# Waits at eleven phase borders of a three-block kernel follow the data in place of the barrier; first products drawn into the phases before

## The reference, cut to what matters

```python
def first_block(x, mem, ...):
    h = _rms(x, attn_norm_g)
    y_fox, y_lru, y_sb, y_mem = ...            # four mixers of h; y_mem attends to mem
    gates = sigmoid(h @ w_in[:, gates] + b_gate)
    mixed = sum over n of gates[n] * (branch[n] @ w_branch[n])
    x = x + mixed @ w_out
    h2 = _rms(x, ffn_norm_g)
    x = x + (silu(conv(h2 @ w_up_gate)) * (h2 @ w_up_val)) @ w_down

def second_block(x, c, ctx, ...):
    for l in range(2):
        mod = silu(c) @ w_ada[l] + b_ada[l]    # shifts, scales and gates, for x and for ctx
        h = modulate(layernorm(x)), hc = modulate(layernorm(xc))
        f = (g_att * (o_att @ w_att_o) + g_gla * (o_gla @ w_gla_o) + g_conv * (y_conv @ w_conv_o)) @ w_out
        x = layernorm(ALPHA * x + gate * f); the same for a gated feed-forward part
```

## Time and profile before

| | us |
|---|---|
| median of 3 runs | 3212.21 (3208.3 to 3212.28) |
| the profiled execution, its device time | 3214.86 |
| span of its trace | 3213.1 |
| TensorE busy in the span | 3066.1 (95%) |
| VectorE busy | 1624.3 (51%) |
| ScalarE busy | 674.1 (21%) |
| mean granted TensorE clock | 0.984 |

### The profile page before, as it was taken

One profiled execution on the slowest core, in us unless ns is written; L12 is line 12 of the kernel. 1 busy time (PEld: TensorE's weight loads), 2 busy tenths in 40 slices (PEclk: granted clock), 3 DMA queues, 4 the chain that ended last, 5 costly groups with the idle time before them and its releaser, 6 DMA issues. The chain is left out here.

```text
span 3213.1 us, 41219 instructions
## 1 busy us (share of the span) xinstructions
PE 3066.1 (95%) x13794; PEld 2429.4 (76%) x13794; DVE 1624.3 (51%) x3320; ACT 674.1 (21%) x1622; POOL 66.9 (2%) x109
## 2 busy tenths in 40 slices
PE   9999899999998999999999999999989999998998
PEld 8888788878885556667775488888856778887887
DVE  4455226656653357658887244445343565753111
ACT  3334220000003333321112132110043431022001
POOL 0000001100110000000000000000000000000000
PEclk9999899999999999999999999999999999999999
DMA  5243347755761011112221202222211223433443
GB/s 187 93 142 101 125 178 266 265 193 203 255 234 53 2 68 54 61 46 85 85 79 65 90 28 83 89 91 85 85 53 42 69 74 111 150 111 111 150 159 103
DMA packets 104999, 363.21 MB, mean 113 GB/s; under 512 B 11489, under 2 KB 17633, under 8 KB 104801
## 3 DMA queue, kind: packets, MB, share of 16 engines
q1 hardware_dynamic: 90832, 310.92, 28.5%
q0 software_dynamic: 14096, 51.39, 4.5%
HBM read 361.21 MB, written 1.05 MB: 113 GB/s over the span
## 5 line engine op out<-in xcount | busy, mean ns | idle before, releaser
L560 PE MATMUL bank<-H,W 128*128 128x256 f32 (+1 forms) x3616 | 879.8, 401 | 9.2 <-DVEq L305 6.3
L560 PEld LDWEIGHTS bank<-H,W 128*128 128x128 f32 x3616 | 690.8, 192 | 177.9 <-issue 85.9
L560 PE MATMUL bank<-YG,W 128*128 128x256 f32 (+1 forms) x1984 | 525.2, 422 | 7.7 <-ACTq L305 7.5
L560 PEld LDWEIGHTS bank<-YG,W 128*128 128x128 f32 x1984 | 378.0, 191 | 137.6 <-issue 94.4
L1031 PE MATMUL bank<-H,W 128*128 128x512 f32 (+1 forms) x320 | 120.4, 513 | 5.4 <-ACT H L1588 5.4
L1128 PE MATMUL bank<-W,H 128*128 128x256 f32 x512 | 117.1, 379 | 0.0
L1300 ACT ACT_TABLE_LOAD x21 | 26.9, 1283 | 391.3 <-DVEq L305 390.2
L880 PE MATMUL bank<-MX,SQ 128*128 128x256 f32 x480 | 105.2, 379 | 0.0
L1128 PEld LDWEIGHTS bank<-W,H 128*128 128x128 f32 x512 | 94.8, 190 | 13.3 <-issue 1.9
L880 PEld LDWEIGHTS bank<-MX,SQ 128*128 128x128 f32 x480 | 91.2, 190 | 12.4
L1031 PEld LDWEIGHTS bank<-H,W 128*128 128x128 f32 x320 | 60.2, 192 | 49.0 <-issue 43.2
(11 more groups left out here) (425 smaller groups left out, 4316.3 us busy)
## 6 DMA issues: line engine op xcount, KB each, us to landing
W<-stream SPq DMA_DIRECT2D x556, 512.0 KB, 3.3
WORK<-ada POOLq DMA_DIRECT2D x59, 512.0 KB, 4.0
SQ<-ada POOLq DMA_DIRECT2D x28, 512.0 KB, 5.0
W<-stream SPq DMA_DIRECT2D x24, 384.0 KB, 3.2
YG<-ada POOLq DMA_DIRECT2D x9, 512.0 KB, 4.5
W<-stream SPq DMA_DIRECT2D x16, 128.0 KB, 2.4
CN<-consts SPq DMA_DIRECT2D x1, 1984.0 KB, 15.4
X<-x_in SPq DMA_DIRECT2D x2, 512.0 KB, 5.0
```

The source lines that it names most:

```text
L560: m = pe.matmul(out_ap, W[u][:, c, :], src[:, c, cols], start=first and c == 0, stop=last and c == k - 1)
```

## The change

TensorE's list `ahead` gets out1, down1, merge2 0, mix_out, conv_norm 1, merge2 1, out2 and down2 1. In each of these the first tile starts after waits on the data themselves (banks that are free, chunks that are written), and `phase_done` is awaited later in the phase. In up2 of layer 0, already in the list, the wait for the last hidden tiles moves behind the first tile. Two first products move across a border that keeps its barrier: the key tiles of memory_first go into stick_last, ahead of each suffix sum, and merge1's first gate tile goes into memory_last, ahead of the transposition; merge1's turns are rotated to match, with the order of the tiles unchanged. `conv_norm` of layer 1 takes the other layer's body. In memory_first the two small products and the root of the context's layernorm move back; its last step moves to merge1's head. VectorE's ada tiles of down1 all go behind the first output tile of a turn.

```diff
@@ stick, memory
                 for k in range(2):
                     project_pair(s, k)
+                    if not s.projects:
+                        memory_key(Step(tally, plan, s.number + 1, 0), k)
                     if s.attends:
...
+            def memory_key(s, u):
+                if u == 0:
+                    pe.wait_ge(*s.before("k_taken"))
+                project(s, u, bank[0][:, u * S:(u + 1) * S], CTX)
...
-                if s.projects:
-                    pe.wait_ge(*s.before("k_taken"))
+                if not s.projects:
+                    first_gate(Step(tally, plan, s.number + 1, 0, counting=False))
+                if s.projects and s.attends:
                     for u in range(2):
-                        project(s, u, bank[0][:, u * S:(u + 1) * S], CTX)
-                        if u == 0 and not s.attends:
-                            ctx_mean(bank[5], ctx_tmp[0], 3)
+                        memory_key(s, u)
...
                     for u in range(2):
                         project(s, 2 + u, bank[1][:, u * S:(u + 1) * S], XS)
-                    if not s.attends:
-                        ctx_mean(bank[6], ctx_tmp[1], 9)
+                        if u == 0 and not s.attends:
+                            ctx_mean(bank[5], ctx_tmp[0], 3)
...
                         project_tokens(s, 4 + u, ...)
+                    if not s.attends:
+                        ctx_mean(bank[6], ctx_tmp[1], 9)
+
+            def first_gate(s):
+                pe.wait_ge(*s.earlier("k_taken", 0))
+                pe.wait_ge(*s.before("gate0"))
+                project(s, 0, bank[0][:, 0:S], XS)
...
+            def merge1_middle(s, following):
+                merge1_rest(s)
+                first_gate(following)
@@ merge2, out_tiles
-                for j in range(2):
-                    pe.wait_ge(*s.before(f"mixed{j}"))
-                    project(s, j, bank[j][:, 0:T2 - cols.start], cols, src=Y2[2])
+                pe.wait_ge(*s.before("mixed0"))
+                pe.wait_ge(*s.done("loaded0"))
+                for c in range(KC):
+                    pe.wait_ge(*s.earlier("conv_done", KC - 1 - c))
+                    m = pe.matmul(bank[0][:, 0:T2 - cols.start], W[0][:, c, :], Y2[2][:, c, cols],
+                                  start=c == 0, stop=c == KC - 1)
+                m.then_inc(*s.tick("unit"))
+                pe.wait_ge(tally.sem("phase_done"), WORKERS * s.number)
+                pe.wait_ge(*s.before("mixed1"))
+                project(s, 1, bank[1][:, 0:T2 - cols.start], cols, src=Y2[2])
...
+                for name in (("gate0", "mixed0", "gate1", "mixed1") if first else ("mixed0",)):
+                    pe.wait_ge(*s.earlier(name, 0))
+                pe.wait_ge(*s.before("added0"))
+                pe.wait_ge(*s.done("loaded0"))
+                for c in range(KC):
+                    if c == KC - 1:
+                        pe.wait_ge(*s.earlier("mixed3" if first else "mixed1", 0))
+                    m = pe.matmul(bank[0][:, 0:S], W[0][:, c, :], MX[:, c, cols], start=c == 0, stop=c == KC - 1)
+                m.then_inc(*s.tick("unit"))
+                for u in range(1, 4):
+                    if u == 2:
+                        pe.wait_ge(tally.sem("phase_done"), WORKERS * s.number)
@@ mix_out, up2, down
+                        if h + i == 0 and c == KC - 1:
+                            pe.wait_ge(*s.earlier("mixed1", 0))
...
-                for i in range(8):
+                pe.wait_ge(*s.earlier("mixed0", 0))
+                out_tile(0, 0)
+                pe.wait_ge(tally.sem("phase_done"), WORKERS * s.number)
+                for i in range(1, 8):
                     out_tile(0, i)
...
-                for j in range(2):
-                    pe.wait_ge(*s.earlier(f"hidden{j}", 0))
...
                     pe.wait_ge(*s.done(f"loaded{j}"))
+                    if j:
+                        for i in range(2):
+                            pe.wait_ge(*s.earlier(f"hidden{i}", 0))
...
+                    if j:
+                        pe.wait_ge(tally.sem("phase_done"), WORKERS * s.number)
+                    else:
+                        pe.wait_ge(*s.earlier("hidden0", 0))
                     for q in range(3):
                         u = 3 * j + q
+                        if u == 2:
+                            pe.wait_ge(*s.earlier("hidden1", 0))
@@ conv_norm_first
-                for name in ("acc_taken0", "first_taken0", "cross_taken0"):
+                for name in (("gate0", "mixed0", "gate1", "mixed1") if s.layer else ("acc_taken0", "first_taken0", "cross_taken0")):
                     pe.wait_ge(*s.earlier(name, 0))
-                for c in range(3):
+                one, two = (1, 3) if s.layer else (3, 5)
+                for c in range(one):
...
@@ ScalarE: memory, condition; VectorE: condition, down1, layernorm
-                    if not s.attends:
-                        ctx_rstd()
                     rstd_pair(s, (1.0, 256 ** -0.5), "q_taken")
...
+                    if not s.attends:
+                        ctx_rstd()
...
-                act.wait_ge(tally.sem("ctx_norm"), 13)
-                act.activation(H[:, :, CTX], ctx_n, ACT.Copy).then_inc(tally.sem("ctx_norm"), 1)
...
+                dve.wait_ge(tally.sem("ctx_norm"), 12)
+                dve.tensor_tensor(H[:, :, CTX], ctx_n, rows(forget_f[:, :]), ALU.mult).then_inc(tally.sem("ctx_norm"), 1)
...
-                    for k in range(2 * j, 2 * j + 2):
+                    for k in range(4 if j == 0 else 0):
                         ada_tile("down1", s.turn, k)
...
-                        dve.tensor_tensor(cen[:, c, c0:T2], cen[:, c, c0:T2], SQ[:, c, c0:T2], ALU.mult)
+                        dve.tensor_tensor(cen[:, c, c0:T2], cen[:, c, c0:T2], SQ[:, c, c0:T2], ALU.mult)\
+                           .then_inc(*s.tick("conv_done"))
```

More of the change, by code:

```diff
@@ L759, in merge, with merge1_begin, merge1_rest @@
+            def merge1_begin(s):
+                pass
+            def merge1_rest(s):
+                for n in range(4):
+                    if n:
+                        pe.wait_ge(*s.before(f"gate{n}"))
+                        project(s, 2 * n, bank[2 * n][:, 0:S], XS)
                     pe.wait_ge(*s.before(f"mixed{n}"))
-                    project(s, 2 * n + 1, bank[2 * n + 1][:, 0:T2 - cols.start], branches[n][1], src=branches[n][0])
-            def merge1(s):
-                merge(s, [(y, slice(0, S)) for y in Y1], XS, 4)
+                    project(s, 2 * n + 1, bank[2 * n + 1][:, 0:S], CTX, src=Y1[n])
@@ L996, in layernorm @@
                 m.then_inc(*s.tick("mean"))
[L997 to L1003, removed]
-                    mean_square(s, bank[1][:, 0:T2 - c0], slice(c0, T2), "variance")
-                if s.plan[s.number][0] == "conv_norm":
-                    for c in range(first_gates, KC):
-                        if c >= 6:
-                            pe.wait_ge(*s.done("gate_conv", c - 6))
-                        project(s, c, bank[2 + c % 6][:, 0:T2 - c0], slice(c0, T2))
+                mean_square(s, bank[1][:, 0:T2 - c0], slice(c0, T2), "variance")
             def attend(s):
@@ L1281, in conv_norm_first @@
+                for c in range(one, two):
+                    project(s, c, bank[2 + c][:, 0:n], cols)
+                mean_pairs(s, bank[1][:, 0:n], cols)
+                for c in range(two, KC):
                     if c >= 6:
                         pe.wait_ge(*s.done("gate_conv", c - 6))
-                    project(s, c, bank[2 + c % 6][:, :], slice(0, T2))
+                    project(s, c, bank[2 + c % 6][:, 0:n], cols)
             run(pe, {"prepare": prepare, "fox": fox, "lru_in": lru_in,
@@ L1286, in _ @@
                      "stick": stick,
-                     "memory": memory, "merge1": merge1, "out1": out_tiles, "norm_ffn1": norm_ffn1, "up1": up,
-                     "down1": down, "ln_mixer": layernorm, "attend": attend,
-                     "gla": (gla_gates, gla_middle, gla_end), "conv": conv, "conv_norm": layernorm, "merge2": merge2,
+                     "memory": memory, "merge1": (merge1_begin, merge1_middle, merge1_rest), "out1": out_tiles,
+                     "norm_ffn1": norm_ffn1, "up1": up, "down1": down, "ln_mixer": layernorm, "attend": attend,
@@ L1290, in _ @@
+                     "gla": (gla_gates, gla_middle, gla_end), "conv": conv, "merge2": merge2,
                      "out2": out_tiles,
                      "post_mixer": layernorm, "ln_ffn": layernorm, "up2": up2, "down2": down, "post_ffn": layernorm, ("down2", 0): down_strassen,
-                     ("conv", 0): conv_strassen, ("conv_norm", 0): conv_norm_first, "mix_out": mix_out},
-                ahead=[("fox_first", 0), ("conv_norm", 0), ("up1", 0), ("attend_first", 0), ("attend_first", 1), ("up2", 0), ("up2", 1)]
+                     ("conv", 0): conv_strassen, "conv_norm": conv_norm_first, "mix_out": mix_out},
@@ L1294, in _ @@
```

(2 more changed lines are left out.)

30 lines of the change are left out of this document (11 added, 19 removed).

## The result

The changed kernel takes 3176.85 us (median of 4 runs, 3175.86 to 3182.09) against 3211.5 of the kernel before (4 runs): a ratio of 0.9891, 95% interval 0.9879 to 0.9904. The forecast was 3176. Its profiled execution took 3177.3 us with a span of 3175.5. Of the title's eleven borders, nine start on waits for data now; into memory_first and merge1 the barrier stays and a first product has moved ahead of it.

A forecast was written before the change was run, and what follows sets the result against it. TensorE, busy 3066.1 of 3213.1 us, was taken to bound the kernel, with its idle time and lower clock. Terms 6.7 + 6.4 + 4.3 + 8.2 + 4.4 + 6.1 = 36.1 us gave a 3176 us median, range 3166 to 3191.

The forecast's parts named there:

- out1: Border from merge1 into out1: 4.0 us of stall and 2.7 of slow clock go, 6.7 us gained.
- down1: Border from up1 into down1: 3.4 us of stall and 3.0 of slow clock go, 6.4 us gained.
- down1 into attend_first: Down1 into ln_mixer: VectorE ends 4.3 us earlier, ScalarE is late; net 6.0 at full clock, 4.3 taken (bounds 1.5 and 6.0).
- stick_last and memory_first: Two key tiles leave memory_first and fill stick_last's stalls: 9.0 us, 8.2 taken for a possible slow stretch (bounds 4.0 and 9.0).
- memory_last and merge1: Gate tile fills memory_last's stall, ending it 0.9 us earlier, and leaves merge1 (3.71): about 4.4 us (bounds 2.8 and 4.6).
- six small borders: mix_out 1.43, up2 of layer 0 0.88, out2 1.17, both merge2 and down2 of layer 1 2.6: together 6.1 us.
- conv_norm 1: conv_norm of layer 1: nothing gained, as its first tile also waits for mixed1, VectorE's last operation; the 2.79 us stall stays.
- the clock does not follow: Rival: slow stretches stay or move to the next stall, only stalls go: 23.5 us gained, 3188.7 us; chance 0.17.
- The rest of a border: TensorE idle time left at each changed border: 0.36 us, taken from conv_norm of layer 0 (bounds 0.2 and 0.6).
- the sign that I named: If right, the timeline at out1, down1, mix_out and merge2 shows 0.3 to 0.5 us idle, ended by issue.
- Added waits: About 125 waits ahead of TensorE's instructions cost nothing; the slower rival had 0.4 us each, 3226 us, chance 0.02.
- late loads: mix_out and out2 have 0.5 us to spare, no wait taken; the rival loses some 4 us, 3180 us, chance 0.05.

The follow-up runs named there:

- the barrier put back: Changed kernel with out1 and down1 taken off TensorE's list, so both wait for the barrier again: 3186.3 us, ratio 0.9916.
- the two borders alone: Kernel before with only out1 and down1 added to TensorE's list, with the new bodies of out_tiles and down: 3198.6 us, ratio 0.9944.
- the experiment with one wait: Changed kernel with conv_norm of layer 1 waiting only for gate0, not for gate0, mixed0, gate1 and mixed1: 3176.6 us.

## Why the prediction was right

Each term is read between fixed points of TensorE's timeline in the two traces (ends of phases, or first matmuls):

| step | forecast | measured |
|---|---|---|
| out1 | 6.7 | 34.65 - 28.63 = 6.0 |
| down1 | 6.4 | 82.54 - 76.77 = 5.8 |
| down1 into attend_first | 4.3 (6.0 at the full clock) | 19.31 - 12.97 = 6.3 |
| stick_last and memory_first | 8.2 (9.0 at the full clock) | 42.63 - 33.17 = 9.5 |
| memory_last and merge1 | 4.4 | 232.01 - 227.48 = 4.5 |
| six small borders | 6.1 | 5.3 |
| conv_norm 1 | 0 | 34.90 - 34.64 = 0.3 |
| sum | 36.1 | 37.7 |

The spans differ by 37.6, the medians by 34.7.

- **The method** held: the barrier's borders, read one by one, and a second price for the clock. Forecast in stalls alone was 23.5 us, measured 24.4; the clock's part was 12.6 by forecast and is 13.2. That these two agree so well is partly chance: the steps of the table hold 23.2 us of stalls and 14.5 of clock, and elsewhere, where nothing was forecast, 1.3 us of clock were lost and 1.2 of idle time gained. The rival "the clock does not follow" is out for the big stalls, by the barrier put back and by the two borders alone. In its looser form it stays true: the same stall is followed by 1.00 or 0.50, and by 0.50 for 3.4 or 6.8 us. The Trainium skill (TensorE: Matmul & The Clock Gate, What's actually happening) says that the monitor's window runs free of the kernel. The traces agree with that in so far as one stall has either clock behind it in different executions; the window itself they do not show.
- **The rest of a border** was mis-sized. "I take 0.36 as the rest at each changed border (bounds 0.2 and 0.6)": it is 0.54 where a loop follows, still inside my bounds, and 0.74 at out1, outside them; and the sign that I named, 0.3 to 0.5 at out1, down1, mix_out and merge2, is met at none of the four (0.74, 0.54, 0.26, 0.54). The row that I had is a border with no loop behind it. This is all of the 0.8 us missing at the small borders, 0.4 of the 0.7 at out1 and 0.2 of the 0.6 at down1.
- **The full-clock time of out1 and down1** was mis-sized too, and is the rest of what is missing there, 0.3 and 0.5 us. I priced their records at 0.215 us each, 27.5 and 75.7 us; at a clock of 1.00 they take 27.9 and 76.2.
- **ln_mixer**: the wait moved to ScalarE's modulation as said (forecast 1.7 and 2.1 us, measured 1.48 and 1.94). The slow stretch that I took half of did come, but behind the 2.11 us before attend_first, so the mean ran at the full clock. The table's step ends ahead of that stretch: its 6.3 is to be held against the 6.0 of the full clock, and with the 1.7 us that attend_first lost it is 4.6, where 4.3 was forecast. That stretch and a second one at the border of attend cost 2.6 us, about what the kernel before lost in two stretches at the end of attend and in attend_last (at 1095 and 1136 us) that are gone, 2.4.
- **memory_first**: the new wait is 1.51 us (forecast 1.6), stick_last ends 2.4 us earlier (forecast 2.1). The terms were set to 8.2 for a slow stretch that did not come in this trace and did in five of ten.
- **memory_last and merge1**: the prediction's own working gives 0.9 + 3.7 = 4.6 us, and its sum has 4.4 without saying why; measured 4.5.
- **conv_norm 1**: 0.3 us, as good as no gain, for the reason given; the experiment with one wait shows it.
- **Added waits and late loads**: nothing, as taken. No tile waits for its load at mix_out or out2.

That the sum came within 1 us of the median is partly luck: three terms were 0.6 to 0.8 too high, two were 1.3 and 2.0 too low as the table has them, and the profiled spans of the same kernel differ by 4 us.

## What to carry to other kernels

When a barrier is loosened, ask of every wait that takes its place whether it guards what the next instructions touch: one superfluous wait kept a whole stall of 2.9 us here, and made that border's change worth nothing. Price a stall twice, by its length and by the clock behind it, and where edits are worth a few us judge them at their place in the timeline and by idle time, which repeated within 0.2 us in the one repeat made here, not by the median, which carries the chance of the clock. What follows a barrier on the other engines (here VectorE's spare work ahead of the last result) can be as good a lever as the barrier: in down1, undoing that order alone cost 5.3 us.

## What the runs showed of the hardware that was not expected

- A restart of TensorE behind its own drain with everything ready costs 0.26 us (merge2 with its first turn peeled); entering a loop, together with waits whose values come from its counter, adds 0.28 (0.54 and 0.26 at merge2 with and without), a wait ahead of the first matmul 0.06 (0.74 and 0.56 at out1 for three).
- The same waits in the middle of a stream of matmuls are free: with 192 more, merge2's busy time is 55.17 and 28.69 us (55.17 and 28.82 without).
- The granted clock behind a given stall is not fixed by the kernel. Busy time of two profiled executions of the same instructions was 3052.9 and 3048.9 us; the first tile of memory_first ran at 1.00 in five traces and began at 0.50 in five, behind the same stalls of 1.25 and 0.98 us. Why a given stall falls one way or the other in a given launch was not settled.
